# A two-block decoder on one core: the even mixer's order, low-rank gates of halves, and the order of shares and maxima in the sparse attention

## The chip, the cores and the metric

One core of one Trainium2 chip runs the whole program in one launch. The metric is the device time of that core in microseconds, the median over runs.

## The reference

Two blocks are computed for 512 tokens of width 1024, batch 1, all in float32. The first has two layers: an even mixer (a gMLP half and a gated delta net half), an MLP of width 4096 with squared relu, a gated addition of a side input, then the same with a differential attention as the mixer. The second has a gated linear attention (GLA) and a sparse attention (NSA). What matters here:

```python
# even mixer: spatial gate, conv + silu of q,k,v, l2 norms, chunked delta rule, out-projection
s = einsum('gts,bnsgc->bntgc', w, layer_norm(v)) + b_s ;  a_out = gelu(u) * s
v_new = u_c - w_c @ state ;  o_c = q_c @ state + qk_c @ v_new ;  state = state * g_last + k_c.T @ v_new
# GLA: a gate of rank 16 (16 columns of the projection, then 16 x 512), heads of 128/256
gk = log_sigmoid(glr @ w_gk_up + b_gk) / 16
o = rms_norm_2(gla_chunked(q, k, v, gk), head_norm) * silu(z) ;  y = o @ w_out
# NSA: per head three softmaxes (compressed keys, selected keys, window), gated and added
o = sum_c gates[c] * softmax(mask_c(q @ k_c.T)) @ v_c ;  y = (o * silu(z)) @ w_out
```

## The kernel before

Every engine has its own hand-ordered program; semaphores join them. Dense products are made of float32r halves: ScalarE rounds a piece of weights to its upper half (`act_weights`, WH), VectorE subtracts to get the lower half (`dve_weights`, WL), and TensorE adds three products (upper x upper, upper x lower, lower x upper) for each pair of tiles. A unit of weights is 1 MB in one of two raw buffers, loaded by the queue of SyncE in the order of `weight_plan`; a unit makes two parts, and a part has one of three WH/WL slots. So part j can be rounded once part j-3 has been used, and the place where `act_weights(a, j)` and `dve_weights(v, j)` stand in the engines' programs decides when it is. `feat` makes 128 output features for all 512 tokens (24 matmuls of 512 columns); `feat_slowly` makes the same in pieces of 8 matmuls, to be put beside other work; `toks` makes 512 output features for the four token tiles, in four PSUM banks. `several` makes a few float32 matmuls into one bank. The eight banks are handed out in turn (`Banks.take`), unless a bank is named, and a bank's next user waits until its last one was read.

The even mixer (`pe_even`, `act_even`, `dve_even`, `pool_even`): ten `qkv` features with convolutions (three VectorE taps each), l2 norms (`pe_l2`, `act_l2`, `dve_l2`), four spatial gates (`pe_gate`, `dve_gate`), two `eu` features, values turned to token form (`vb`), the products `at` and `qk` with `dve_products`, then five doubling levels of an inverse (jobs `m` and `xy`, lines 1134 to 1158) with pieces of dense features beside them (`beside`), and a recurrence of four chunks n, into which `gm_product` puts the eight out-projections of the gMLP half. `head_norm`, `head_square`, `head_scale`, `head_gain`, `head_half` and `head_rest` finish a chunk's output. The second out-projection is `eo`, and the norm ahead of the MLP (`act_norm`, `dve_norm`) follows.

GLA (`pe_gla`, `act_gla`, `dve_gla`, `pool_gla`): the 16 gate columns are the job `gs`, copied to `GLR`; four float32 matmuls with 16 rows (`gup`) widen them. Per head h there are state updates (`values`), outputs, and `finish_head`, which sums two tiles of squares by two float32 matmuls with ones (lines 2122, 2123).

NSA (`pe_nsa`, `act_nsa`, `dve_nsa`, `pool_nsa`): 52 units u in two halves f; token tile q is 3, 2, 1, 0, and each (f, q) starts with one unit on compressed keys (branch None), then units on selected and window keys. In step i TensorE makes scores(i+2), turns shares(i) and multiplies values(i-1), and in the first half three steps of four also hold a dense piece. ScalarE copies half of the turned shares and makes the exponentials (i+2). VectorE's step (line 2914) is

```python
nsa_step(i, ((most, 2), (scale, 1), (turn_, 0), (mix, -1)))
```

that is, the row maxima of unit i+2, then the factors (gate over sum) of unit i+1, then its copy of half of turned unit i, then the mixing where a q ends; `split_` follows, and in some steps `z_gate` with a part of weights. GpSimd waits for the factors and multiplies the shares of unit i+1 (`share`), and TensorE's `turn_` waits for that. At the end the out-projection `yo` takes banks 0 to 3 and then 4 to 7, while the last three steps still run.

## Time and profile before

| what | value |
|---|---|
| median of 3 runs | 2063.66 us (2061.76 to 2064.04) |
| the profiled execution's own time | 2062.59 us |
| its span | 2060.4 us |
| mean granted TensorE clock | 0.996 |
| TensorE busy | 1980.1 us, 96% of the span |
| VectorE, ScalarE, GpSimd busy | 1069.3, 891.7 and 221.5 us |

The span is shown in stretches by stage: the even mixer takes about 16 to 314 us, GLA 1407 to 1650 us, NSA 1650 to the end. PE is TensorE, DVE VectorE, ACT ScalarE, POOL GpSimd. A float32 matmul counts as two instructions.

### The profile page before, as it was taken

How to read it: one execution, taken by the hardware profiler on the slowest of the kernel's cores; microseconds unless marked ns; L12 is line 12 of the kernel's file. 1: busy time of each engine (PE TensorE's matmuls, PEld its weight loads, DVE VectorE, ACT ScalarE, POOL GpSimd, SP SyncE). 2: the span in 40 equal slices, each digit the busy share in tenths (PEclk: the TensorE clock that was granted, in tenths of full speed). 3: DMA queues.
4: the chain of work that ended last, by engine and by line, in shares of the span. 5: the costliest groups of instructions: out<-in, count | busy, mean ns of one | idle time of the engine just before them, and what ended most of it. 6: DMA issues, size and time to landing. Idle time of an engine off the chain costs nothing.

```text
span 2060.4 us, 27307 instructions
## 1 busy us (share of the span) xinstructions
PE 1980.1 (96%) x11161; PEld 1592.5 (77%) x11161; DVE 1069.3 (52%) x1706; ACT 891.7 (43%) x1659; POOL 221.5 (11%) x225
## 2 busy tenths in 40 slices
PE   7999989999999999999999999999999989999888
PEld 6778878888888788656888888887887778966567
DVE  5576555434434552566543434356535656555763
ACT  5562244323223563666442323256434442355562
POOL 1011000000000000342000000000000034233440
PEclk9999999999999999999999999999999999999999
DMA  4221013333232322111332333223221155611002
GB/s 146 81 76 48 22 62 99 96 102 101 84 102 82 102 77 97 62 41 42 93 103 85 99 102 102 82 83 97 82 92 62 62 149 147 177 42 42 1 1 72
DMA packets 122945, 169.94 MB, mean 82 GB/s; under 512 B 7562, under 2 KB 83862, under 8 KB 122822
## 3 DMA queue, kind: packets, MB, share of 16 engines
q1 hardware_dynamic: 114966, 151.00, 23.2%
q0 software_dynamic: 5504, 14.58, 2.6%
q10 hardware_dynamic: 2352, 2.62, 0.4%
q8 instruction: 89, 1.46, 0.3%
q14 instruction: 34, 0.28, 0.0%
HBM read 158.22 MB, written 2.10 MB: 78 GB/s over the span
## 4 chain that ended last, share of the span: by engine, by line
PE 78%; DVE 9%; ACT 7%; issue 2%; POOL 1%; DMA 1%; DVEq 0%; SPq 0%; ACTq 0%
PE PSUM L520 59%; PE PSUM L558 6%; PE PSUM L528 5%; DVE WL L413 2%; ACT XN L430 2%; PE PSUM L535 2%; ACT WH L486 1%; ACT TM L430 1%; DVE AR L413 1%; ACT AR L430 1%; PE PSUM L2557 1%; DVE AR L421 1%; PE PSUM L2606 1%; DVE XL L413 1%; PE PSUM L2578 1%
## 5 line engine op out<-in xcount | busy, mean ns | idle before, releaser
L413 DVE TENSOR_TENSOR WL<-RAW,WH 128x1024 fp32r<-128x1024 f32 (+2 forms) x284 | 348.9, 1230 | 383.7 <-ACT WH L486 383.2
L486 ACT CAST WH<-RAW 128x1024 fp32r<-128x1024 f32 (+2 forms) x284 | 293.2, 1035 | 372.2 <-PE PSUM L520 366.5
L520 PE MATMUL PSUM<-XH,WH 128*128 128x512 f32 (+3 forms) x1120 | 414.9, 370 | 10.5 <-DVE XL L413 6.7
L520 PE MATMUL PSUM<-XH,WL 128*128 128x512 f32 (+3 forms) x1120 | 407.3, 364 | 0.0
L520 PE MATMUL PSUM<-XL,WH 128*128 128x512 f32 (+3 forms) x1120 | 407.2, 364 | 0.0
L520 PE MATMUL PSUM<-WH,HP 128*128 128x512 f32 x1024 | 318.0, 390 | 1.9 <-DVE WL L413 1.9
L520 PE MATMUL PSUM<-WH,XH 128*128 128x512 f32 (+2 forms) x608 | 239.1, 393 | 11.7 <-DVE WL L413 5.5
L520 PEld LDWEIGHTS PSUM<-XH,WH 128*128 128x128 f32 (+2 forms) x1120 | 209.3, 187 | 50.7 <-DVE XL L413 8.4
L520 PEld LDWEIGHTS PSUM<-XL,WH 128*128 128x128 f32 (+2 forms) x1120 | 209.3, 187 | 35.8 <-issue 2.9
L520 PEld LDWEIGHTS PSUM<-XH,WL 128*128 128x128 f32 (+2 forms) x1120 | 209.0, 187 | 34.1
L520 PE MATMUL PSUM<-WH,XL 128*128 128x512 f32 (+2 forms) x608 | 232.0, 382 | 0.0
L520 PE MATMUL PSUM<-WL,XH 128*128 128x512 f32 (+2 forms) x608 | 231.6, 381 | 0.0
L520 PEld LDWEIGHTS PSUM<-WH,HP 128*128 128x128 f32 x1024 | 192.2, 188 | 42.7 <-DVE WL L413 2.8
L430 ACT ACTIVATE TM<-PSUM 128x512 f32<-128x512 f32 x128 | 76.0, 598 | 312.0 <-PE PSUM L520 259.3
L520 PE MATMUL PSUM<-WL,HP 128*128 128x512 f32 x512 | 199.2, 389 | 0.0
L520 PEld LDWEIGHTS PSUM<-WH,XH 128*128 128x128 f32 x608 | 115.1, 189 | 39.0 <-DVE WL L413 8.1
L413 DVE TENSOR_TENSOR TM<-TM 128x512 f32<-128x512 f32 x70 | 48.5, 692 | 169.1 <-ACT TM L430 168.4
L520 PEld LDWEIGHTS PSUM<-WL,XH 128*128 128x128 f32 x608 | 115.2, 189 | 22.2 <-issue 2.2
L520 PEld LDWEIGHTS PSUM<-WH,XL 128*128 128x128 f32 x608 | 114.9, 189 | 21.9
L520 PEld LDWEIGHTS PSUM<-WL,HP 128*128 128x128 f32 x512 | 96.1, 188 | 19.8
L528 PE MATMUL PSUM<-AR 64*64 64x64 f32 (+6 forms) x1424 | 97.9, 260 | 7.6 <-ACT TM L430 3.5
L528 PEld LDWEIGHTS PSUM<-AR 64*64 64x64 f32 (+3 forms) x1424 | 74.4, 149 | 29.7 <-issue 20.1
(236 smaller groups left out, 2480.4 us busy)
## 6 DMA issues: line engine op xcount, KB each, us to landing
RAW<-in_w_mlp_dram SPq DMA_DIRECT2D x64, 1024.0 KB, 5.2
RAW<-in_nsa_w_in_dram SPq DMA_DIRECT2D x13, 1024.0 KB, 5.5
RAW<-in_w_in_e_dram SPq DMA_DIRECT2D x12, 1024.0 KB, 5.2
RAW<-in_w_qkv_o_dram SPq DMA_DIRECT2D x12, 1024.0 KB, 5.2
RAW<-in_gla_w_in_dram SPq DMA_DIRECT2D x12, 1024.0 KB, 5.3
RAW<-in_w_ple_gate_dram SPq DMA_DIRECT2D x8, 1024.0 KB, 5.0
RAW<-in_w_out_e_dram SPq DMA_DIRECT2D x4, 1024.0 KB, 5.0
RAW<-in_w_out_o_dram SPq DMA_DIRECT2D x4, 1024.0 KB, 5.0
```

Of the source, the lines that this page charges most:

```text
L413: return x.do.tensor_tensor(o, a, b, op)
L421: return x.do.scalar_tensor_tensor(out=o, in0=a, scalar=s, in1=b, op0=op0, op1=op1)
L430: return a.do.activation(o, i, func, **kw)
L486: a.do.copy(hi, r).then_inc(*up("w_hi", "w_hi", j))
L520: m = p.do.matmul(o, l, r, start=start and i == 0, stop=stop and i == len(pairs) - 1)
L528: m = p.do.matmul(o, l, r, start=True, stop=True)
L535: m = p.do.transpose(o, i, IDT[0:i.shape[0], 0:i.shape[0]])
L558: m = p.do.matmul(PS[bank], l, r, start=i == 0, stop=i == len(pairs) - 1)
L2557: p.do.matmul(o[r][:, nk * j:nk * j + nk], NQ[h, m0 + j, cs], (KS, KW)[br][h, (m0 + j) // 2, 0:nk], start=j == 0, stop=False, skip_group_c ...
L2578: x = p.do.transpose(o[:, 128 * (c * n + j):128 * (c * n + j) + 128], NSB[u % 3][:, r, nk * j + 128 * c:nk * j + 128 * c + 128], IDT)
L2606: x = p.do.matmul(o[64 * r:64 * r + 64, 128 * l:128 * (l + w)], (VS, VW)[br][:, c, 64 * g:64 * g + 64], PT[u % 2][:, r, 128 * (c * n + j): ...
```

## The change

Six places are edited; all else is the same.

1. Even mixer, gates: gate 3 goes behind the first `eu` feature, the two `eu` features take the named banks of qkv(2,3) and qkv(2,2), and the `vb` turns go behind both. VectorE takes gate 3 and the first product with `gu` ahead of `vb`.
2. Even mixer, levels: the eighteen pieces are dealt out so that level 5 has two between `m` and `xy`; the weights behind the last feature go behind the splits of the gMLP half.
3. Even mixer, recurrence: at n = 1 ScalarE rounds weights ahead of `head_scale`; VectorE's `head_gain` goes behind the next chunk's `RR`; the last products are put around `head_norm(2)`. In `eo`, weights are split up to one part less, but earlier.
4. GLA gate: the 16 columns are loaded three times, at 0, 32 and 64 of 80 columns; `UP` is cleared by GpSimd and loaded three times; ScalarE rounds both; VectorE subtracts to get `UPH[64:80]` and `GLR[32:48]`; the four `gup` matmuls are float32r with 80 rows.
5. GLA heads: VectorE adds the two tiles of squares, one matmul with ones is left, and `finish_head(h)` goes behind the next head's first `gz`.
6. NSA: `scale` ahead of `most`; the out-projection in other banks.

Semaphore names are also merged (`v_spread`, `v_stats`, `dt_a_log`, `gate_halves`), with the same waits.

```diff
-    S(w, 2048, 2064)
+    plan.append(("R", rows(w)[:, :, 2048:2064]))
...
+                if plan[u][0] == "R":
+                    for i in range(3):
+                        load(s, f"raw{u % NR}", ("raw", u) if i == 2 else (), raw_of(u)[:, :, 32 * i:32 * i + 16], plan[u][1])
+                    continue
...
-                if i in (8, 9):
-                    for g in (2 * i - 16, 2 * i - 15):
-                        pe_gate(p, g)
-            feat(p, ("eu", 0), EVEN)
+                if i == 8:
+                    pe_gate(p, 0)
+                    pe_gate(p, 1)
+                elif i == 9:
+                    pe_gate(p, 2)
+            feat(p, ("eu", 0), EVEN, bank=ps.where["qkv", 2, 3][0])
+            pe_gate(p, 3)
+            feat(p, ("eu", 1), EVEN, bank=ps.where["qkv", 2, 2][0])
             for n in range(4):
                 p.wait_ge(*at("qkv", 2, 3))
                 pe_token_form(p, "vb", n, VT)
-            feat(p, ("eu", 1), EVEN)
...
                     pe_token_form(p, "kd", lv - 1, KN)
+                else:
+                    beside(2)
...
-                if lv <= 4:
-                    beside(3 if lv == 1 else 2)
+                beside((2, 2, 2, 1, 0)[lv - 1])
...
-                gm_product()
-                if n:
-                    head_norm(n - 1)
+                if n < 3:
+                    gm_product()
+                    if n:
+                        head_norm(n - 1)
                 within(n)
+            head_norm(2)
+            gm_product()
             head_norm(3)
...
+                if n == 1:
+                    act_weights(a, first_part["eg", 0] + 4)
+                if n == 3:
+                    head_square(3)
                 if n:
                     head_scale(n - 1)
-                if n == 1:
-                    act_weights(a, first_part["eg", 0] + 4)
-            head_square(3)
...
                     for t in range(4):
                         act_half(a, MLP0, t)
+                        if t == 1:
+                            act_weights(a, j + 3)
...
             dve_gate(v, 2)
-            dve_gate(v, 3)
             dve_l2(v, 1, range(4))
...
             dve_weights(v, first_part["eu", 0] + 3)
+            dve_gate(v, 3)
+            gate(0)
             for n in range(4):
                 dve_token_form(v, "vb", n, VB, beta)
-            gate(0)
...
-                if lv == 4:
-                    dve_weights(v, first_part["ez", 3] + 3)
...
+                    if n > 1:
+                        head_gain(n - 2)
                     gm_add(*adds.pop(0))
...
                     for t in range(4):
                         add(t)
+                        if t == 2:
+                            dve_weights(v, j + 3)
                         dve_half(v, MLP0, t)
-                    dve_weights(v, j + 4)
...
-                several(p, ("gup", h), lambda b: [(b[:, :], UP[:, 128 * h:128 * h + 128], GLR)])
+                several(p, ("gup", h), lambda b: [(b[:, :], UPH[:, 128 * h:128 * h + 128], GLR)])
...
             def finish_head(h):
-                p.wait_ge(*at("gsq", h, 1))
-                b = ps.take("gn", h)
-                p.wait_ge(*ps.empty("gn", h))
-                p.do.matmul(PS[b][:, :], ONE, tm("gq", h, 0), start=True, stop=False)
-                p.do.matmul(PS[b][:, :], ONE, tm("gq", h, 1), start=False, stop=True).then_inc(*ps.filled("gn", h))
+                p.wait_ge(*at("gsq_sum", h))
+                several(p, ("gn", h), lambda b: [(b[:, :], ONE, tm("gq", h, 0))])
...
                     feat(p, ("gz", 2 + 2 * h), GLA)
+                    if h:
+                        finish_head(h - 1)
                     feat(p, ("gz", 3 + 2 * h), GLA)
                     values(h + 1)
                 outputs(h)
-                if h < 3:
-                    finish_head(h)
+            finish_head(2)
...
+            a.wait_ge(*at("gk_up"))
+            a.do.copy(UPH, UP).then_inc(*up("gate_halves", "up_hi"))
+            a.wait_ge(*ps.full("gs"))
+            a.do.copy(GLR, bank("gs")[0:80, :]).then_inc(*up("gate_halves", "glr_hi"))
...
+            g.wait_ge(*ps.full("pg", 1, 0, 0))
+            step(g, g.do.memset(UP, 0.0))
+            for i in range(3):
+                load(g, "gk_up", ("gk_up",) if i == 2 else (), UP[32 * i:32 * i + 16, :], I["gla_w_gk_up_2"][0])
...
-                 tiles=TILES[1], banks=(0, 1, 2, 3))
-            toks(p, ("yo", 1, 1), mixed_ready, tail=True, tiles=TILES[1], banks=(4, 5, 6, 7))
+                 tiles=TILES[1], banks=(2, 1, 0, MORE))
+            toks(p, ("yo", 1, 1), mixed_ready, tail=True, tiles=TILES[1], banks=(ACC, 5, 4, 3))
...
-                nsa_step(i, ((most, 2), (scale, 1), (turn_, 0), (mix, -1)))
+                nsa_step(i, ((scale, 1), (most, 2), (turn_, 0), (mix, -1)))
```

## Rows read from the trace of the kernel before

**Rows 1.** The page: the span, and busy time of TensorE (share, instructions).

```profile
span 2060.4 us, 27307 instructions
PE 1980.1 (96%) x11161; PEld 1592.5 (77%) x11161; DVE 1069.3 (52%) x1706; ACT 891.7 (43%) x1659; POOL 221.5 (11%) x225
```

**Rows 2.** Waits of TensorE, whole span: total us, times, longest.

```profile
PE PSUM L2578 <- POOL AR L413: 12.3, 19, 1.5
```

**Rows 3.** Stretches: us, busy PE, PEld, DVE, ACT, POOL, PEclk, DMA share, GB/s.

```profile
140.50:143.90 3.40, 3.25 (x9) 2.48 (x8) 2.65 (x5) 3.31 (x7) 0.00 (x0) 0.50 0.02 5
300.90:304.30 3.40, 3.40 (x10) 2.63 (x9) 1.17 (x2) 1.94 (x5) 0.00 (x0) 0.50 0.93 291
1441.00:1444.40 3.40, 3.40 (x9) 2.64 (x8) 0.90 (x2) 3.35 (x7) 0.00 (x0) 0.50 0.01 4
```

**Rows 4.** Gates to products: one stretch, then timeline of PE and DVE (start, us).

```profile
136.02:155.03 19.01, 15.41 (x73) 12.85 (x73) 13.65 (x17) 11.47 (x14) 0.00 (x0) 0.91 0.32 102
...
139.48 1.18 PE L528 MATMUL PSUM<-AR 128*128 128x128 f32 x8 [3.45 <-ACT TM L430]
...
134.45 2.32 DVE L421 SCALAR_TENSOR_TENSOR AR<-PSUM,COL,AR 128x511 f32<-128x511 f32 x3
...
168.15 0.43 DVE L413 TENSOR_TENSOR AR<-CS,AR 128x256 f32<-128x256 f32 x1
```

**Rows 5.** Timeline of PE, levels and recurrence of the even mixer.

```profile
227.81 7.37 PE L528 MATMUL PSUM<-AR 64*64 64x64 f32 x192 [1.20 <-DVE AR L413]
...
262.25 0.50 PE L520 MATMUL PSUM<-WH,XH 128*128 128x512 f32 x1 [1.76 <-DVE WL L413]
...
265.37 1.16 PE L528 MATMUL PSUM<-AR 128*128 128x128 f32 x8 [1.46 <-DVE AR L413]
...
283.85 1.12 PE L528 MATMUL PSUM<-TM,CB 128*128 128x512 f32 x2 [1.03 <-ACT TM L430]
```

**Rows 6.** Timeline of PE, out-projection `eo` and first MLP features; last, ACT.

```profile
299.63 0.50 PE L520 MATMUL PSUM<-WH,XH 128*128 128x512 f32 x1 [2.37 <-DVE WL L413]
299.96 0.39 PE L520 MATMUL PSUM<-WL,XH 128*128 128x512 f32 x1
300.19 0.40 PE L520 MATMUL PSUM<-WH,XL 128*128 128x512 f32 x1
...
314.85 0.36 PE L520 MATMUL PSUM<-XH,WH 128*128 128x256 f32 x1 [0.79 <-DVE XL L413]
...
313.85 1.04 ACT L486 CAST WH<-RAW 128x1024 fp32r<-128x1024 f32 x1
```

**Rows 7.** GLA gate: timeline of PE, then the DMA issue of its columns.

```profile
1436.80 3.69 PE L528 MATMUL PSUM<-AR 16*128 16x512 f32 x8
...
RAW<-in_gla_w_in_dram SPq DMA_DIRECT2D x1, 64.0 KB, 3.8
```

**Rows 8.** Timeline of PE, end of the first GLA head.

```profile
1555.48 1.13 PE L2122 MATMUL PSUM<-TM,CB 128*128 128x512 f32 x2 [0.69 <-ACT TM L430]
1556.44 1.02 PE L2123 MATMUL PSUM<-TM,CB 128*128 128x512 f32 x2
```

**Rows 9.** Timeline of one NSA step, second half, q 3: DVE, ACT, POOL, PE.

```profile
1937.21 1.99 DVE L413 TENSOR_TENSOR XL<-TM,XH 128x512 fp32r<-128x512 f32 x1
1939.13 1.21 DVE L2853 TENSOR_REDUCE ST<-PSUM 128x2 f32<-128x1024 f32 x1
1940.26 0.15 DVE L2885 RECIPROCAL ST<-ST 128x2 f32<-128x2 f32 x1
...
1936.45 0.69 ACT L430 ACTIVATE AR<-PSUM,ST 128x512 f32<-128x512 f32 x1 [0.38 <-DVE ST L2853]
...
1936.77 1.89 POOL L413 TENSOR_TENSOR AR<-AR,ST 128x1024 f32<-128x1024 f32 x1 [2.03 <-DVE ST L413]
...
1938.71 1.09 PE L2578 MATMUL PSUM<-CB,AR 128*128 128x128 f32 x8 [0.52 <-POOL AR L413]
```

**Rows 10.** Timeline of PE, start of NSA's out-projection.

```profile
2005.45 0.50 PE L520 MATMUL PSUM<-WH,XH 128*128 128x512 f32 x1 [2.81 <-ACT AR L430]
```

More of the change, by code:

```diff
@@ L1322, in z_gate @@
                 act(a, EZ[:, m, :], bank("ez", m)[:, :], ACT.Silu).then_inc(*ps.read("ez", m))
-                act_weights(a, first_part["ez", m] + 3)
+                if m < 3:
+                    act_weights(a, first_part["ez", m] + 3)
             def gate(m):
@@ L1347, in act_even @@
                     step(a, act(a, va, va, ACT.Ln, scale=1.0 / 128, bias=EPSC))
-                    act(a, va, va, ACT.Exp, scale=-0.5).then_inc(*up("v_scale", "v_scale"))
+                    act(a, va, va, ACT.Exp, scale=-0.5).then_inc(*up("v_spread", "v_scale"))
                     conv_silu(j, m)
@@ L2050, in bass_decoder_pair @@
         RS = CS[:, L_R:L_R + 512]
-        UP = slot(11)[0:16, 0:512]
-        GLR = slot(11)[0:16, 512:1024]
+        UP = slot(3)[0:80, 0:512]
+        UPH = PP[0:80, 0, 0, :]
+        GLR = PP[0:80, 0, 1, :]
+        SECOND, THIRD = slice(32, 48), slice(64, 80)
         PI = slot(11)[:, 1024:1536].bitcast(I32)
@@ L2209, in act_gla @@
                     gz(2 + 2 * h)
+                    if h:
+                        finish_head(h - 1)
                     gz(3 + 2 * h)
                 outputs(h)
-                if h < 3:
-                    finish_head(h)
                 if h == 2:
-                    for m in range(6):
+                    for m in range(4):
                         place(m)
             j = first_part["yo", 0, 0]
+            finish_head(2)
+            place(4)
+            place(5)
             finish_head(3)
@@ L2255, in dve_gla @@
             dve_weights(v, first_part["gs",] + 2)
-            v.wait_ge(*ps.full("gs"))
-            v.do.tensor_copy(GLR, bank("gs")[0:16, :]).then_inc(*ps.read("gs"))
+            v.wait_ge(*at("up_hi"))
+            tt(v, UPH[THIRD, :], UP[THIRD, :], UPH[THIRD, :].bitcast(F32), ALU.subtract).then_inc(*up("up_lo", "up_lo"))
+            v.wait_ge(*at("glr_hi"))
+            tt(v, GLR[SECOND, :], bank("gs")[SECOND, :], GLR[SECOND, :].bitcast(F32), ALU.subtract).then_inc(*ps.read("gs"))
             dve_weights(v, first_part["gs",] + 5)
@@ L2331, in values, with sum_squares @@
                 book.put(("g_state", h), f"bank{ps.where[job][0]}_read", ps.where[job][1])
+            def sum_squares(h):
+                v.wait_ge(*at("gsq", h, 0))
+                v.wait_ge(*at("gsq", h, 1))
+                tt(v, tm("gq", h, 0), tm("gq", h, 0), tm("gq", h, 1), ALU.add).then_inc(*up("gsq_sum", "gsq_sum", h))
             def finish_head(h):
@@ L2348, in dve_gla @@
                     gz(2 + 2 * h)
+                    if h:
+                        finish_head(h - 1)
                     gz(3 + 2 * h)
                     values(h + 1)
-                    finish_head(h)
+                sum_squares(h)
                 if h == 2:
-                    for m in range(6):
+                    for m in range(4):
                         place(m)
@@ L2373, in dve_gla @@
             j = first_part["yo", 0, 0]
+            finish_head(2)
+            place(4)
+            place(5)
             finish_head(3)
```

34 lines of the change are left out of this document (19 added, 15 removed).

## Prediction

> **What bounds the kernel now.** I read the page first: TensorE is busy 1980.1 of 2060.4 us [rows 1], so the kernel is TensorE's own work plus 80 us in which it stands still. A change can gain in three ways only: a wait of TensorE that goes, work of TensorE that goes, or a stretch at the lower clock that goes. Next I read TensorE's waits. The largest entry is 12.3 us in 19 waits for GpSimd [rows 2], all in the sparse attention. The rest I took one by one from TensorE's timeline, at the places that the diff touches; each row shows the idle time before it and what ended it. Last I read stretches for the granted clock. Three of 3.4 us show 0.50, which is 1.2 of 2.4 GHz [rows 3]: one behind 3.45 us of standing still, one behind 2.37 us, and one behind four matmuls that use 16 rows [rows 4, 6, 7]. At 0.50 half of the work of 3.4 us is lost, so each costs 1.7 us.
>
> **Even mixer, gates.** Gate 3 waited 3.45 us for ScalarE to read the l2 sum in its bank [rows 4]. Now the first `eu` feature stands ahead of it, in the bank of qkv(2,3), whose last reader is VectorE's third tap, which ends at 134.45 + 2.32 = 136.77 [rows 4]. TensorE was free at 136.02, so it waits 0.8 us. That takes 2.65 us off the stretch of 19.01 us [rows 4], and with a wait that short I expect the slow stretch behind it to go too, 1.7 us: 4.35. The second `eu` feature needs the bank of qkv(2,2), which is also gate 2's, read long before. VectorE doesn't gain as much: ahead of its products stand the same splits, four `vb` tiles and now gate 3 and one product. It gains about 3.2 us, and GpSimd's products with the decays come at the same time. Its last diagonal was ready at 168.6 [rows 4], some 0.7 us ahead of TensorE; TensorE being 4.35 us earlier, a new wait of 0.5 to 1 us arises. I take 0.8: net 3.5 us.
>
> **Levels.** The second half of level 5 waited 1.20 us for VectorE's masked product [rows 5], which was held behind a split of weights. Two pieces of 8 matmuls now lie between, 16 x 0.23 = 3.7 us by the spacing 299.96 to 300.19 [rows 6], and the split has gone behind. The wait goes: 1.2 us. They are taken from ends of levels 1 and 4, where two pieces and one remain, enough for VectorE's subtraction. The upper halves of the gMLP part begin later, as the last feature ends later, but behind them TensorE has 7.37 us of small matmuls [rows 5]: nothing.
>
> **Recurrence.** At n = 2 TensorE waits 1.76 us for lower halves and then 1.46 us for `RR` [rows 5]. Both come from ScalarE, which loaded a table and scaled head 0 before it rounded, and from VectorE, which took the gain of head 0 before `RR`. Turned about, both are on time; head 0's scale is 2 us later, and nothing waits for it until its place in the out-projection. At n = 3 the square of head 3 was waited for 1.03 us [rows 5]; a product of 2.7 us (12 x 0.23) now lies between. Sum 4.2 us.
>
> **Out-projection `eo`.** TensorE waited 2.37 us for the split of its last part, and the stretch at 0.50 follows [rows 6, 3]: 2.37 + 1.7 = 4.1 us. The price: the first part of the MLP was split here as well, and now isn't. ScalarE rounds it only behind its second turned tile, at 313.85 for 1.04 us [rows 6], VectorE then takes about 1.2 us, to 316.15, where TensorE began at 314.85 after 0.79 us [rows 6]. So 1.3 us comes back, and as 2.1 us of standing still may again be followed by the slow clock, I put 0.4 more. Net 2.4 us. Even mixer in all: 3.5 + 1.2 + 4.2 + 2.4 = 11.3 us.
>
> **GLA gate.** Four float32 matmuls took 3.69 us [rows 7]; as float32r of 512 columns they take 4 x 0.23 = 0.92. That is 2.8 us, and the slow stretch that follows them [rows 3] should go, as 80 rows now work: 1.7 us. Against it: rounding and splitting the gate columns takes 640 elements, not 128, on ScalarE and VectorE in the norm, where ScalarE is always busy. The bounds are nothing and the 1.04 us of a full part [rows 6]; by length 0.5 more, which I take in full. GpSimd's clearing of `UP` and two more loads lie on a queue that had nothing else to do in the MLP. SyncE issues three loads where one of 64 KB landed in 3.8 us [rows 7]; even in a row they end in 11.4 us, and a raw buffer is filled two units ahead, four parts or some 22 us of TensorE's work (4 x 24 x 0.23): nothing. Net 4.0 us.
>
> **GLA heads.** After each of three heads TensorE waited 0.69 us for the squares, then ran two matmuls, 0.96 us from start to start [rows 8]; by a `gup`, 3.69 / 4, I take 0.9 for one [rows 7]. Now a feature of 5.5 us covers squares and VectorE's addition, and one matmul is left: 3 x 0.69 + 4 x 0.9 = 5.7 us. With `finish_head(2)` behind head 3, outputs(3) loses 2.5 us of cover for VectorE's seven state updates and may wait 0.8 us; a wait of as much for the first split halves ahead of the out-projection goes in turn. Net 5.6 us. GLA: 9.6 us.
>
> **Sparse attention.** One step of the second half at q = 3 shows the ring. GpSimd's share runs 1936.77 to 1938.66, VectorE's XL subtraction beside it takes 1.99 us and ends at 1939.20, then come 1.21 us of maxima, 0.4 us of factors, and the next share at about 1940.7: 3.9 us [rows 9]. TensorE waits 0.52 us in it [rows 9], so alone it needs 3.4. With factors ahead of maxima, GpSimd starts 1.2 us earlier and the wait goes, if a new ring stays below 3.4: maxima 1.21, two exponentials 2 x 0.69, factors 0.4, signals 0.1, or 3.1 us [rows 9]. It does, barely. It doesn't where the exponentials are eight short ones, or where the compressed unit's four operations stand between; there some 0.8 us may stay at each of four changes of q without dense pieces. So of 12.3 us [rows 2] I take 9.5. The out-projection's first tile used bank 3 and waited 2.81 us for the last exponentials [rows 10]; in bank 7 it doesn't, and tiles 2, 1 and 0 come late enough: 2.8 us. NSA: 12.3 us.
>
> A VectorE subtraction of two SBUF tiles takes 1.99 us beside a share and ends just behind it [rows 9]. The Trainium skill, GPSIMD Engine Reference, section Specifications, says that GpSimd's SBUF interfaces are shared with VectorE, with contention for instructions with two SBUF inputs; the trace agrees. By that rule the change can lose: shares that start earlier fall on the compressed unit's subtraction, as the first rival has it.
>
> **Sum.** 11.3 + 9.6 + 12.3 = 33.2 us off the profiled execution's 2062.59 us: 2029.4. That execution is 1.1 us under the median, so I forecast 2031 us.
>
> **Rivals.**
> - *A: GpSimd holds VectorE.* The share now lies beside the maxima of the compressed unit and the splits, and those that read two SBUF tiles are stretched by up to 1.3 us (1.99 against 0.7) [rows 9], so the next maxima are late and TensorE waits as long as before. For it: the 1.99. Against it: maxima and copies read PSUM and keep their length. Only the 2.8 is gained: 2063.7 - 11.3 - 9.6 - 2.8 = 2040 us.
> - *B: new waits in the mixers.* Half of 20.9 us comes back, in VectorE's products, at state 3, before the MLP: 2063.7 - 10.4 - 12.3 = 2041 us. A and B together: 2051.
> - *C: everything goes well.* No residue at the changes of q (2.8 more), none in `eo` (1.7): 2026.
> - *D: slower.* VectorE now waits for the exponentials of unit i+1 before the maxima of i+2. If ScalarE's copy (about 0.6) and the share itself (1.89) come to stand in this ring, because the factors wait on both, a step takes 1.21 + 1.38 + 0.4 + 0.1 + 0.6 + 1.89 = 5.6 us against 3.9 [rows 9], 1.7 more in each of the 26 steps of the second half: 44 us. 2063.7 - 23.7 + 44 = 2084 us. It decides from 0.9 us a step (23.7 / 26). Against it: a share ends in TensorE's step before the factors of the next but one are wanted.
> - *E: no effect*, as TensorE's waits and clock only move: 2063.
>
> **How the numbers follow.** Forecast 0.55 (2027 to 2036 by its own terms), A 0.13, B 0.12, A and B 0.04, C 0.10, D 0.04, E 0.02. The range 2022 to 2046 takes in the forecast, A, B and C, 0.9 of the chance, which allows for sizes misjudged. Faster by over 0.2% (4.1 us, about what can be told from no change here) is 0.94, within it 0.02, slower 0.04.
>
> **What would show it.** In the profile after: no wait over 1 us before gate 3, clock 1.00 there and behind `gup`; `gup` 0.9 us; no wait at level 5 or n = 2; a wait of about 2 us before the first MLP feature; no GpSimd waits at q = 3 in the second half, and under 3 us of them in all; the out-projection starting without one. If TensorE's waits for GpSimd stay near 12 us, A holds; if VectorE waits for exponentials in most steps and steps take over 3.9 us, D does.

## The result, and the profile after

The changed kernel takes 2026.42 us (median of four, 2025.94 to 2026.63) against 2062.71 us before in the same comparison: a ratio of 0.9825, with a 95% interval of 0.9808 to 0.9842. Its profiled execution took 2026.30 us, with a span of 2024.5 us. The forecast was 2031 us, in a range of 2022 to 2046.

The page after, its span and busy times, to be held against [rows 1]:

```profile
span 2024.5 us, 27299 instructions
PE 1967.3 (97%) x11149; PEld 1589.8 (79%) x11149; DVE 1069.7 (53%) x1711; ACT 893.3 (44%) x1661; POOL 223.2 (11%) x228
```

Of the 35.9 us by which the span is shorter, 12.8 are busy time of TensorE and 23.1 are time in which it stood still. The other engines do as much as before: it is all order, four shorter matmuls, four left out, and the clock.

TensorE's waits after (total us, times, longest). The first line answers to [rows 2]:

```profile
PE PSUM L526 <- DVE WL L413: 9.1, 10, 2.8
...
PE PSUM L2624 <- POOL AR L413: 4.2, 7, 1.0
...
PE PSUM L2603 <- ACT AR L430: 1.3, 2, 0.7
```

12.3 us in 19 waits for GpSimd have become 4.2 us in 7; two waits for ScalarE at the scores are new.

To see where the rest came off, I laid the two PE timelines beside each other and took the time between the same matmul in both, at points where the work is the same. The distance grows from 0.5 us at 118 us (the first transfers, which vary from run to run) to 14.8 us at the end of the first MLP norm's first wait (314.85 before, 300.02 after), of which 1.4 are given back in the next 350 us, since at 0.50 the start of the MLP is slower here. It is 13.4 us all through the MLPs and the odd mixer, 23.5 us from the linear attention's out-projection to the sparse attention's features (1669.99 and 1646.50), and 35.9 at the end. Less the 0.5 us at 118 us, the even mixer gave 12.9 us, the linear attention 10.1, the sparse attention 12.4; forecast were 11.3, 9.6 and 12.3.

Four stretches of the trace after (columns as in [rows 3]):

```profile
139.00:142.40 3.40, 3.40 (x18) 2.85 (x18) 2.04 (x4) 3.33 (x6) 0.00 (x0) 1.00 0.00 0
...
300.68:304.09 3.41, 3.41 (x19) 3.41 (x18) 2.66 (x5) 3.31 (x8) 0.00 (x0) 0.50 0.39 90
1424.00:1428.00 4.00, 4.00 (x19) 3.31 (x18) 2.92 (x4) 1.90 (x3) 0.00 (x0) 1.00 0.80 262
1635.30:1638.71 3.41, 3.41 (x19) 3.41 (x18) 3.31 (x5) 3.31 (x7) 0.00 (x0) 0.50 0.00 0
```

The first and the third are the places of the gates and of `gup`, where the clock was 0.50 before [rows 3] and is 1.00 now. Half clock stands in two others: behind the wait for the first MLP feature, and at the start of the sparse attention. The second costs nothing. The next wait behind it, for VectorE's lower halves, is shorter by as much (PE timelines before and after):

```profile
1669.99 0.36 PE L520 MATMUL PSUM<-XH,WH 128*128 128x256 f32 x1 [1.19 <-DVE XL L413]
...
1646.50 0.36 PE L526 MATMUL PSUM<-XH,WH 128*128 128x256 f32 x1 [0.50 <-DVE XL L413]
```

From the end of the wait of 2.78 us ahead of the stretch to these matmuls it is 12.60 us before, all at full clock, and 12.62 us after, with 3.41 us at 0.50.

The PE timeline after, at the places of [rows 4 to 7], with VectorE's split at 298.55 and its tap at 133.99 between:

```profile
136.45 0.47 PE L526 MATMUL PSUM<-XH,WH 128*128 128x512 f32 x1 [0.88 <-DVE AR L421]
...
133.99 2.32 DVE L421 SCALAR_TENSOR_TENSOR AR<-PSUM,COL,AR 128x511 f32<-128x511 f32 x3
...
164.66 0.68 PE L534 MATMUL PSUM<-CB,AR 64*64 64x64 f32 x16 [0.26 <-DVE AR L413]
...
231.12 0.50 PE L526 MATMUL PSUM<-WH,XH 128*128 128x512 f32 x1 [1.42 <-DVE XL L413]
...
300.02 0.36 PE L526 MATMUL PSUM<-XH,WH 128*128 128x256 f32 x1 [2.08 <-DVE WL L413]
...
298.55 1.22 DVE L413 TENSOR_TENSOR WL<-RAW,WH 128x1024 fp32r<-128x1024 f32 x1
...
1423.71 1.09 PE L534 MATMUL PSUM<-PP 80*128 80x512 f32 x4
1424.64 0.40 PE L526 MATMUL PSUM<-XH,WH 128*128 128x512 f32 x1
...
1575.70 0.49 PE L2135 MATMUL PSUM<-AR 128*128 128x128 f32 x2 [0.76 <-DVE AR L421]
```

Gate 3's 3.45 us are down to 0.88 us, behind VectorE's third tap, which ends at 136.31. The new wait for VectorE's products is 0.26 us. The waits of 1.20, 1.76, 1.46, 1.03 and 2.37 us [rows 5, 6] have no successor; what is left there is 1.42 us at 231.12, which stood before as well (at 236.60), and 2.08 us before the MLP. The four `gup` matmuls take from 1423.71 to 1424.64, 0.93 us. The third state of the linear attention is waited for 0.76 us.

One step of the sparse attention in the second half at q = 3 (timelines of POOL, DVE and PE), and the first matmul of its out-projection, which answer to [rows 9, 10]:

```profile
1903.19 1.89 POOL L413 TENSOR_TENSOR AR<-AR,ST 128x1024 f32<-128x1024 f32 x1 [1.18 <-DVE ST L413]
1906.27 1.89 POOL L413 TENSOR_TENSOR AR<-AR,ST 128x1024 f32<-128x1024 f32 x1 [1.18 <-DVE ST L413]
...
1904.77 0.86 DVE L413 TENSOR_TENSOR XL<-TM,XH 128x512 fp32r<-128x512 f32 x1
...
1906.10 1.22 DVE L2899 TENSOR_REDUCE ST<-PSUM 128x2 f32<-128x1024 f32 x1
...
1903.09 1.09 PE L2652 MATMUL PSUM<-AR 128*64 128x128 f32 x16
...
1906.27 1.09 PE L2652 MATMUL PSUM<-AR 128*64 128x128 f32 x16
...
1969.48 0.50 PE L526 MATMUL PSUM<-WH,XH 128*128 128x512 f32 x1
```

Shares start every 3.07 to 3.08 us, and TensorE's step takes 3.18; before, both took 3.92. No wait stands in the step, and none before the out-projection.

### The profile page after: what moved, and what is told of

The parts are those of the page before. It is cut to its first block, busy times and chain, and to the rows that moved or that the text cites. A ratio compares the mean times of both kernels' runs of the same rounds, so it can differ in the third digit from the quotient of the medians.

```text
span 2024.5 us, 27299 instructions
## 1 busy us (share of the span) xinstructions
PE 1967.3 (97%) x11149; PEld 1589.8 (79%) x11149; DVE 1069.7 (53%) x1711; ACT 893.3 (44%) x1661; POOL 223.2 (11%) x228
## 3 DMA queue, kind: packets, MB, share of 16 engines
q8 instruction: 89, 1.46, 0.3%
## 4 chain that ended last, share of the span: by engine, by line
PE 80%; DVE 9%; ACT 7%; issue 3%; DMA 0%; SPq 0%; DVEq 0%; ACTq 0%
PE PSUM L526 63%; PE PSUM L564 5%; PE PSUM L534 5%; ACT AR L430 2%; ACT XN L430 2%; DVE AR L413 1%; PE PSUM L541 1%; DVE WL L413 1%; DVE AR L421 1%; DVE ST L2899 1%; ACT WH L492 1%; ACT TM L430 1%; PE PSUM L2603 1%; DVE XL L413 1%; PE PSUM L2652 1%
## 5 line engine op out<-in xcount | busy, mean ns | idle before, releaser
L526 PE MATMUL PSUM<-XH,WH 128*128 128x512 f32 (+3 forms) x1120 | 415.0, 371 | 13.4 <-DVE XL L413 6.1
L413 POOL TENSOR_TENSOR AR<-AR,ST 128x1024 f32<-128x1024 f32 (+2 forms) x52 | 81.5, 1567 | 135.9 <-DVE ST L413 135.9
L534 PE MATMUL PSUM<-AR 64*64 64x64 f32 (+5 forms) x1416 | 93.9, 258 | 0.8 <-ACT AR L1418 0.8
```

Source lines behind the costliest of these rows:

```text
L413: return x.do.tensor_tensor(o, a, b, op)
L526: m = p.do.matmul(o, l, r, start=start and i == 0, stop=stop and i == len(pairs) - 1)
L534: m = p.do.matmul(o, l, r, start=True, stop=True)
```

## The experiments

Every kernel below is the changed one with the edit shown. They were run in three groups, each beside the kernel before: the two NSA orders, the old banks and the early split (before: 2065.32 us), the four mixer edits put back (2064.33), and the changed kernel once more with the split in the gap, both improvements and the compressed-unit order in old banks (2064.65). Differences to the changed kernel are taken from its 2026.42 or 2026.18 us. Those between groups carry some uncertainty: the kernel before moved from 2062.71 to 2065.32 between them. The profiles also differ from the changed kernel's first one by -1.1 to +0.9 us at 22 us already, where no edit has come into play, so where a cost is read from two traces, I take it inside the edited stage, from the same matmuls in both.

### The changed kernel once more

> The changed kernel itself, once more, as the measure for the three beside it on the same chip, and to see which of its 3.4 us stretches at half clock stay where they are. In the ten profiles read so far, TensorE stands still before the first MLP feature for 2.1 us in eight, and a stretch at 0.50 follows in five of these. Theory 1: whether one follows a wait is chance; then the five runs show mean clocks that differ by up to 0.002 and times that differ by one or two times 1.7 us, 2026 to 2030 us. Theory 2: it is fixed by the kernel: the stretches stand at about 300.7, 1635.3 and at the end again, and all times agree within 1 us.

2026.18 us (2025.97 to 2027.56, four runs), ratio 0.9819 (0.9806 to 0.9833). Two stretches of its trace:

```profile
231.78:235.19 3.41, 3.41 (x10) 2.66 (x9) 0.18 (x1) 0.40 (x2) 0.00 (x0) 0.50 0.00 0
300.68:304.09 3.41, 2.74 (x23) 2.77 (x24) 3.19 (x6) 2.26 (x6) 0.00 (x0) 1.00 0.03 8
```

The same kernel with the same waits (1.42 and 2.06 us) has its half clock behind the first of them this time, and full clock behind the second. The stretch at 1634.66 is in both. So the place isn't fixed by the kernel, though the sum hardly differs: theory 1 holds for the place, and the times lie within 1.6 us, not much more than the 1 us of theory 2. Over the fourteen profiles of this study the stretch behind the 1.42 us wait is there in seven. The wait of 2.1 us before the first MLP feature stands in ten of them, and a stretch follows in six; in nine of these ten exactly one of the two places has it. The Trainium skill, TensorE: Matmul & The Clock Gate, Part 1, says of a kernel's start that the number of slow matmuls differs between runs of one kernel. These two traces show the like in the middle of a kernel: 19 matmuls at 0.50 from 300.68 us in one, 10 from 231.78 us in the other.

### Maxima first again, new banks kept

```diff
-                nsa_step(i, ((scale, 1), (most, 2), (turn_, 0), (mix, -1)))
+                nsa_step(i, ((most, 2), (scale, 1), (turn_, 0), (mix, -1)))
```

> The changed kernel with one line put back: in the sparse attention VectorE takes the maxima of unit i+2 before the factors of unit i+1 again; the new banks of the out-projection stay. My theory: the order alone gave 9.5 us in the prediction, and in the trace TensorE's waits for GpSimd fell from 12.3 to 4.2 us while 1.3 us of new waits for ScalarE at the scores came up, so 7 to 9.5 us come back: 2033.5 to 2036 us, with waits of about 0.5 us for GpSimd at every step of q = 3 in the second half. Rival: the banks were what counted (the exponentials' banks come free earlier), and the order alone is worth under 3 us: 2027 to 2029 us.

2035.82 us (2035.29 to 2036.46), 9.4 us over the changed kernel. The spans (2034.7 and 2024.5) differ by 10.2, but 0.8 of it stands at 22 us already; inside the sparse attention it is 9.4, with 0.63 at a wait for lower halves at 1727 that this order doesn't explain. VectorE's split of a mixed tile at q = 3 takes 2.00 us again, at 1914.35. Its waits for GpSimd:

```profile
PE PSUM L2624 <- POOL AR L413: 12.5, 19, 1.5
```

The 19 waits are back to the count, and my theory holds: it said 7 to 9.5 us. A wait costs more than its own length: TensorE's step is 3.92 us with 0.53 of waiting and 3.18 without.

### The old banks, new order kept

```diff
-                 tiles=TILES[1], banks=(2, 1, 0, MORE))
-            toks(..., tiles=TILES[1], banks=(ACC, 5, 4, 3))
+                 tiles=TILES[1], banks=(0, 1, 2, 3))
+            toks(..., tiles=TILES[1], banks=(4, 5, 6, 7))
```

> The changed kernel with the out-projection's banks put back, tiles 3, 2, 1, 0 in banks 3, 2, 1, 0 and then 7, 6, 5, 4; the order of factors and maxima stays. My theory: its first tile waits 2.8 us again for the last exponentials to be read, nothing else moves, and a wait of that length may be followed by 3.4 us at half clock, 1.7 us more: 2029 to 2031 us. Rival: with the factors ahead of the maxima the last exponentials are early enough, and the banks are worth under 1 us: 2026.4 to 2027.4 us.

2034.11 us (2033.66 to 2034.30), 7.7 us over the changed kernel, and 8.0 by the traces, all of it inside the sparse attention. I expected 2.8 to 4.5. PE and DVE timelines, then the stretch:

```profile
1975.78 0.80 PE L526 MATMUL PSUM<-WH,XH 128*128 128x512 f32 x1 [5.62 <-ACT AR L430]
...
1966.98 1.23 DVE L2899 TENSOR_REDUCE ST<-PSUM 128x8 f32<-128x1024 f32 x1
```

```profile
1972.76:1979.59 6.83, 3.81 (x9) 3.05 (x10) 1.00 (x4) 3.41 (x17) 3.29 (x3) 0.50 0.01 3
```

The wait is 5.62 us, not the 2.81 of [rows 10], and 6.83 us at half clock go with it, of which 3.8 are work (1.9 lost; with 5.62 that is 7.5 of the 8.0). VectorE takes the factors of the last compressed unit (1965.50 to 1967.07) ahead of the maxima at 1966.98, and so the exponentials behind them are late. That is a price of the new order which I had not seen, and the new banks hide it. Both theories fall.

### Maxima first at the compressed units only

```diff
+                if i + 1 < NT and n_at[i + 1][2] is None:
+                    nsa_step(i, ((most, 2), (scale, 1), (turn_, 0), (mix, -1)))
+                else:
+                    nsa_step(i, ((scale, 1), (most, 2), (turn_, 0), (mix, -1)))
-                nsa_step(i, ((scale, 1), (most, 2), (turn_, 0), (mix, -1)))
```

> The changed kernel, but where unit i+1 is a compressed one (the first of each q, its factors are four operations of VectorE behind one of GpSimd's share) the maxima of i+2 stand ahead of the factors again; everywhere else the factors stand ahead. Theory 1: the 0.94 us for which TensorE waits at 1898, just behind a compressed unit, comes from maxima that are held behind these four operations; ahead of them they are 1.9 us earlier, and some 0.5 us are gained at each of three or four changes of q: 2024.4 to 2026 us. Theory 2: TensorE turns the compressed unit itself before the next one, so what is gained there is lost at its own turn, which now waits 0.6 us for its share: 2026 to 2028 us. Theory 3: the order of the compressed units was as much of the gain as the rest: 2029 us or more.

2024.23 us (2023.98 to 2024.68), 2.0 to 2.2 under the changed kernel, and faster than either order taken throughout. The two were not run side by side; inside the sparse attention the traces differ by 2.1. Its waits for GpSimd:

```profile
PE PSUM L2624 <- POOL AR L413: 1.5, 2, 1.0
...
PE PSUM L2619 <- POOL AR L413: 0.9, 2, 0.6
```

4.2 us have become 2.4. Theory 1 holds, with a little more than it asked; of theory 2 there are two waits, 0.31 and 0.59 us, for the compressed unit's own share. The wait of 1.04 us at 1892, behind eight short exponentials, stays.

### The same with the old banks

The edit of the section before, and `banks=(0, 1, 2, 3)` and `banks=(4, 5, 6, 7)` in the out-projection.

> The sparse attention with maxima ahead only where unit i+1 is a compressed one, and the out-projection in the old banks. It tells why the banks were worth 5.6 us of waiting with the new order, and 2.8 us with the old. My theory: with the factors ahead everywhere the maxima of the last unit but one stand behind the four operations of the compressed unit, and the last exponentials end 5.6 us behind the point where TensorE wants their bank; with maxima ahead there, they end at 1971.9 us where TensorE is free at 1967.9 us in the trace with the new banks, so it waits 4.0 us, and 3.4 to 6.8 us at half clock may follow: 2030 to 2032.5 us. Rival: the wait is set by the number of exponentials alone and stays 5.6 us: 2032 to 2034 us.

2030.13 us (2028.79 to 2031.27). The out-projection's first matmul:

```profile
1971.60 0.79 PE L526 MATMUL PSUM<-WH,XH 128*128 128x512 f32 x1 [3.86 <-ACT AR L430]
```

3.86 us where I had worked out 4.0, in place of 5.62. My theory holds: 1.8 us of the wait came from the maxima behind the compressed unit. What is left over the 2.81 of before, 1.05 us, is the order as well, in the last step, as the last scores and the maxima of these scores show (PE and DVE, this kernel, then before):

```profile
1965.66 0.60 PE L2606 MATMUL PSUM<-CS 128*128 128x512 bf16 x2
1967.07 0.20 DVE L2931 RECIPROCAL ST<-ST 128x8 f32<-128x8 f32 x1 [0.93 <-ACT AR L430]
1967.39 1.22 DVE L2899 TENSOR_REDUCE ST<-PSUM 128x8 f32<-128x1024 f32 x1
...
2000.52 0.60 PE L2560 MATMUL PSUM<-CS 128*128 128x512 bf16 x2
2001.23 1.22 DVE L2853 TENSOR_REDUCE ST<-PSUM 128x8 f32<-128x1024 f32 x1 [0.20 <-PE PSUM L2560]
```

Before, the maxima start 0.71 us after the start of the last scores' matmuls. Here they start 1.73 us after it, since the factors of the unit before stand ahead of them and wait for its exponentials. That is 1.02 of the 1.05 us. Maxima first in the last step too, with the old banks, was not run. Here too 6.83 us at half clock stand by the wait.

### The first MLP split, one addition too early

```diff
                            dve_weights(v, j + 3)
                        dve_half(v, MLP0, t)
+                    dve_weights(v, j + 4)
```

> The changed kernel, and VectorE also splits the first part of the MLP's weights behind the fourth addition of the first half of the even mixer's out-projection, where it stands still for 1.35 us and ScalarE has rounded that part 1.2 us before. My theory: the wait of 2.08 us before the first MLP feature is this split alone; it falls to the 0.7 us that the second turned tile's lower halves set, and the stretch at half clock behind it goes as well, 1.7 us: 2.6 to 3.1 us less, 2023.3 to 2023.8 us. Rival 1: the wait shrinks but the stretch at half clock stays, as at other places it also follows waits that are no longer than this: 1.3 us less, 2025.1 us. Rival 2: VectorE is late by one split with the norm of the first tiles and the wait only changes its cause: 2026 to 2027 us.

2027.41 us (2025.42 to 2032.53), just past the 2026 to 2027 of rival 2, and four executions that spread by 7 us decide little; so I go by the trace, which is of the fastest. PE, then DVE:

```profile
291.85 1.09 PE L541 MATMUL PSUM<-CB,XN 128*128 128x128 f32 x8 [1.86 <-ACT XN L430]
...
287.90 1.23 DVE L413 TENSOR_TENSOR WL<-RAW,WH 128x1024 fp32r<-128x1024 f32 x1 [0.79 <-ACT WH L492]
```

Rival 2: of the wait before the MLP 0.49 us is left, but the addition stands behind the split, at 289.04, the first tile's scale behind the addition, and TensorE waits 1.86 us for that.

### The same split in VectorE's gap

```diff
                    tt(v, o, o, bank("eo", c, t)[:, :], ALU.add).then_inc(*ps.read("eo", c, t))
+                    if c and t == 0:
+                        dve_weights(v, j + 2)
```

> The changed kernel, and VectorE splits the first part of the MLP's weights right behind the first addition of the second half of the even mixer's out-projection. One addition earlier the same split only exchanged a wait of 2.08 us before the first MLP feature for one of 1.86 us before the first turned tile, as the addition was late. Theory: in the gap of 1.35 us in which VectorE waits for the first tile's scale the 1.22 us cost nothing; the wait falls to about 0.8 us, that is 1.3 us less than the kernel beside it, and 3.0 us less where the stretch at half clock behind it goes as well. Rival: the split is still too long for the gap, the first tile is turned later, and the waits together stay near 2 us: within 0.5 us of it.

2024.03 us (2023.01 to 2024.69), 2.15 under the changed kernel beside it. PE, then DVE:

```profile
299.00 0.36 PE L526 MATMUL PSUM<-XH,WH 128*128 128x256 f32 x1 [0.77 <-DVE XL L413]
...
287.67 1.22 DVE L413 TENSOR_TENSOR WL<-RAW,WH 128x1024 fp32r<-128x1024 f32 x1
289.10 0.49 DVE L417 TENSOR_SCALAR XN<-H,ST 128x512 f32<-128x512 f32 x1 [0.22 <-ACT ST L430]
```

The split ends at 288.89, before the scale is there, and the wait is 0.77 us. That is 1.3 us; the other 0.85 lies between nothing and the 1.7 of one stretch, of which this trace has one less than the changed kernel's.

### Both improvements

> The changed kernel with two more edits: VectorE takes the maxima ahead of the factors where unit i+1 is a compressed one (alone its profile was 1.6 us shorter, with 2.4 us less of waiting for GpSimd), and it splits the first part of the MLP's weights behind the first addition of the second half of the out-projection. Theory: the two lie in different stages and add up: 1.3 to 3 us for the split and 1.6 to 3 us for the order, 3 to 6 us less than the changed kernel beside it. Rival: what is saved at the waits comes back as stretches at half clock at other places: under 2 us less.

2021.74 us (2020.37 to 2022.30, five runs), ratio 0.9795 (0.9782 to 0.9808), 4.4 us under the changed kernel beside it and 42.9 under the kernel before. The single gains were 2.0 and 2.15: they add up. Beside the split alone, run in the same group, the order of the compressed units gives 2.3 us, so that gain doesn't rest on a comparison between groups. This is the fastest version found.

### The gates put back

```diff
-                if i == 8:
-                    pe_gate(p, 0)
-                    pe_gate(p, 1)
-                elif i == 9:
-                    pe_gate(p, 2)
-            feat(p, ("eu", 0), EVEN, bank=ps.where["qkv", 2, 3][0])
-            pe_gate(p, 3)
-            feat(p, ("eu", 1), EVEN, bank=ps.where["qkv", 2, 2][0])
+                if i in (8, 9):
+                    for g in (2 * i - 16, 2 * i - 15):
+                        pe_gate(p, g)
+            feat(p, ("eu", 0), EVEN)
...
+            feat(p, ("eu", 1), EVEN)
...
             dve_gate(v, 2)
+            dve_gate(v, 3)
...
-            dve_gate(v, 3)
-            gate(0)
             for n in range(4):
                 dve_token_form(v, "vb", n, VB, beta)
+            gate(0)
```

> The changed kernel with the even mixer's gates put back: all four gates ahead of the first eu feature, the eu features in banks of their own choice, VectorE's value tiles ahead of its first gate product. My theory: the wait of 3.45 us ahead of gate 3 comes back for the two short ones that stand there now (0.88 and 0.26 us), 2.3 us, and with it the stretch at half clock behind it, 1.7 us: 4.0 us, 2030 to 2031 us. Rival: a stretch at half clock belongs to the work in it (small matmuls), not to the wait ahead, and is not changed by this: 2.3 us, 2028.5 to 2029 us.

2032.22 us (2031.65 to 2033.01), 6.0 us over the changed kernel. PE timeline, and two stretches:

```profile
138.54 0.71 PE L534 MATMUL PSUM<-AR 128*128 128x128 f32 x4 [3.44 <-ACT TM L430]
```

```profile
139.35:142.76 3.41, 3.41 (x11) 2.60 (x10) 2.55 (x4) 3.31 (x6) 0.00 (x0) 0.50 0.00 0
234.92:238.33 3.41, 3.41 (x10) 2.64 (x9) 0.71 (x1) 0.93 (x3) 0.00 (x0) 0.50 0.00 0
```

The wait of 3.44 us and the half clock behind it are both back, as my theory has it, which said 2.3 + 1.7 = 4.0. The second stretch is the one that the changed kernel has sometimes here, sometimes at the MLP. Inside the even mixer this kernel loses 4.1 us by the traces. The median of 2032.22 is over the theory's 2030 to 2031 us all the same. In the profile a further 1.7 us are lost in the sparse attention, at two waits in code that the edit doesn't touch: 0.89 us at 1730.20 for VectorE's lower halves and 0.57 us at 1771.54 for ScalarE. They come and go between profiles: the changed kernel's two have neither, the first stands in four others with 0.32 to 0.71 us, and the profile before has both. Why stays open.

### The low-rank gate put back

The core of the edit; the loads, GpSimd's clearing and ScalarE's copies go back with it.

```diff
-    plan.append(("R", rows(w)[:, :, 2048:2064]))
+    S(w, 2048, 2064)
...
-        UP = slot(3)[0:80, 0:512]
-        UPH = PP[0:80, 0, 0, :]
-        GLR = PP[0:80, 0, 1, :]
+        UP = slot(11)[0:16, 0:512]
+        GLR = slot(11)[0:16, 512:1024]
...
-                several(p, ("gup", h), lambda b: [(b[:, :], UPH[:, 128 * h:128 * h + 128], GLR)])
+                several(p, ("gup", h), lambda b: [(b[:, :], UP[:, 128 * h:128 * h + 128], GLR)])
...
-            tt(v, GLR[SECOND, :], bank("gs")[SECOND, :], GLR[SECOND, :].bitcast(F32), ALU.subtract)...
+            v.do.tensor_copy(GLR, bank("gs")[0:16, :]).then_inc(*ps.read("gs"))
```

> The changed kernel with the low-rank gate of the linear attention put back: four float32 matmuls with 16 rows, one copy of VectorE, loads of 16 rows and columns. My theory: the four matmuls take 3.7 us again in place of 0.9, the stretch at half clock behind them comes back (1.7 us), and the 0.42 us that rounding and splitting cost in the norm goes: 4.1 us, 2030 to 2031 us. Rival 1: the stretch at half clock came from the waits of the norm before it and does not come back: 2.4 us, 2028.5 to 2029 us. Rival 2: the features behind the gate wait for VectorE or ScalarE, which cover the longer matmuls: under 1.5 us, 2026 to 2028 us.

2031.22 us (2030.78 to 2033.13), 5.0 over. PE timeline and stretch:

```profile
1423.68 4.20 PE L528 MATMUL PSUM<-AR 16*128 16x512 f32 x8
```

```profile
1426.75:1433.58 6.83, 6.83 (x16) 4.51 (x15) 3.44 (x7) 6.65 (x12) 0.00 (x0) 0.50 0.15 52
```

The profiled execution is the slowest of the four (2033.13). From 1393 to 1609 us it loses 5.6 us. 6.83 us at half clock cost 3.4, the four matmuls 2.8, and 0.4 come back in the norm, where the wait of 0.78 us before the gate columns is gone. Rivals 1 and 2 fall; the half clock behind these matmuls is as real as I took it, and here twice as long. It starts while they run, and TensorE's last wait, of 1.06 us, ended at 1407.33, 19 us earlier. Whether the 16 rows bring it, or the float32 format and the 3.7 us that come with them, isn't shown: the edit changes all three.

### Two matmuls for a head's norm

```diff
-                p.wait_ge(*at("gsq_sum", h))
-                several(p, ("gn", h), lambda b: [(b[:, :], ONE, tm("gq", h, 0))])
+                p.wait_ge(*at("gsq", h, 1))
...
+                p.do.matmul(PS[b][:, :], ONE, tm("gq", h, 0), start=True, stop=False)
+                p.do.matmul(PS[b][:, :], ONE, tm("gq", h, 1), start=False, stop=True)...
...
-                sum_squares(h)
```

> The changed kernel, but the norm of each of the four heads of the linear attention sums its two halves with two accumulating matmuls again, and VectorE does not add them first; the place of the norm, behind the next feature, stays. It tells the two parts of that edit apart. My theory: each matmul left out is worth 0.9 us, as the prediction has it by the float32 matmuls of the gate: 3.6 us, less up to 0.5 us of waits that VectorE's additions cause: 2029.5 to 2030.2 us. Rival: beside a feature's matmuls the second one takes its columns at the full rate, 0.23 us each: 0.9 us, 2027.3 us.

2030.62 us (2029.59 to 2031.10), 4.4 over. By the PE timelines 3.5 us of it lie between 1407 and 1609 us, 0.88 for each of the four:

```profile
1543.62 1.02 PE L2148 MATMUL PSUM<-TM,CB 128*128 128x512 f32 x2
1544.48 1.02 PE L2149 MATMUL PSUM<-TM,CB 128*128 128x512 f32 x2
```

The 0.9 us holds, and the rival's 0.23 doesn't. So of the 5.6 us forecast for the heads, 3.5 are matmuls; the 2.1 for the covered squares rest on the three waits of 0.69 us that are gone [rows 8], and were not run by themselves. The 0.9 us between 3.5 and 4.4 lie outside this stretch and belong to nothing that I found.

### The recurrence put back

The core of the edit, for TensorE (the third product and the norm of head 2), ScalarE and VectorE:

```diff
-                if n < 3:
-                    gm_product()
-                    if n:
-                        head_norm(n - 1)
+                gm_product()
+                if n:
+                    head_norm(n - 1)
...
-                if n == 1:
-                    act_weights(a, first_part["eg", 0] + 4)
                 if n:
                     head_scale(n - 1)
+                if n == 1:
+                    act_weights(a, first_part["eg", 0] + 4)
...
-                    if n > 1:
-                        head_gain(n - 2)
...
+                if n:
+                    head_gain(n - 1)
```

> The changed kernel with the recurrence of the even mixer put back: ScalarE loads and scales before it rounds at n = 2, VectorE takes the gain of the head before ahead of the residual, the third product and the norm of head 2 in their old place. My theory: three waits of 1.76, 1.46 and 1.03 us come back, 4.2 us: 2030 to 2031 us. Rival 1: as TensorE now comes to this part relatively earlier against the other engines, the waits are longer and one of them is followed by 3.4 us at half clock: 2032 us or more. Rival 2: the wait of 2.08 us before the first MLP feature takes part of them in, since the norm that it waits for is no later: 2027 to 2029 us.

2034.48 us (2034.37 to 2034.63), 8.3 over. PE timeline and stretch:

```profile
256.26 0.50 PE L526 MATMUL PSUM<-WH,XH 128*128 128x512 f32 x1 [1.76 <-DVE WL L413]
...
259.38 0.58 PE L534 MATMUL PSUM<-AR 128*128 128x128 f32 x1 [1.26 <-DVE AR L413]
...
280.23 0.70 PE L534 MATMUL PSUM<-TM,CB 128*128 128x512 f32 x1 [1.04 <-ACT TM L430]
```

```profile
257.60:264.43 6.83, 5.57 (x25) 5.05 (x24) 2.29 (x4) 1.59 (x3) 0.00 (x0) 0.50 0.40 150
```

The three waits are back, 4.1 us, no longer than before, and half clock with them, 6.83 us with 5.57 us of work, of which half is lost, 2.8. So of rival 1, which gave 2032 us or more, the half clock holds and the longer waits don't. Up to the first MLP feature this kernel loses 7.5 us, so 0.6 are left, or 0.2 for each wait, by an estimate. The kernel before had much the same waits without half clock. So the edit is worth 4.1 us by its waits, and 2.8 more where it also keeps the clock up.

## Why the prediction was right

**Even mixer, gates.** Right in kind and nearly in size. The wait before gate 3 is 0.88 us (0.8 forecast), the stretch is gone, and putting the order back costs both. The new wait at the products is 0.26 us, not 0.8: VectorE had more room than I gave it.

**Levels and recurrence.** No wait at level 5, at n = 2 or at n = 3. The levels' edit was not run by itself; its 1.2 us rests on the two traces. The recurrence's waits measured 4.1 us against the 4.2 of the forecast.

**`eo`.** The 2.37 us went and 2.08 us stand before the MLP, as worked out (0.79 + 1.3). That the split of the first MLP part is the whole of it is shown by its place in VectorE's gap, where 0.77 us are left. I counted 0.4 for the slow clock behind it; it came in one of two profiles of the same kernel, at the price of the stretch at 231, which stood in the profile before as well and which I left out of the sum. The profile before also has half clock at 236, where it costs 1.4 us by the two timelines, and the changed kernel's first profile hasn't; the half clock at the MLP costs 1.4 us and not the 0.4 put down for it. So of the 1.6 us by which 12.9 is over 11.3, 0.4 are these two, 0.5 are the products, and 0.7 are booked to no wait. This stage came out near the forecast partly by luck, since the clock's place isn't fixed.

**GLA.** Forecast 9.6 us, measured 10.1, term by term: `gup` 0.93 us for 0.92; the norm 0.4 us longer for 0.5 (from 1407.08 to 1420.44 before, 13.36 us; from 1393.61 to 1407.39 after, 13.78 us); a head's matmul 0.88 for 0.9; the wait at outputs(3) 0.76 for 0.8. The stretch behind `gup` is gone, and comes back with the old matmuls; the reason that I gave for it, that 80 rows work in place of 16, isn't shown by itself.

**Sparse attention.** 12.4 us for 12.3, but the two terms are not what I said they were. Inside this stage, the order undone costs 9.4 us (9.5 forecast), the banks undone 8.0 (2.8 forecast). So of the 12.4 the order alone would have given 4.4 and the banks alone 3.0; these two are differences, and neither was run. The step that failed is the one that took the out-projection's 2.81 us as independent of the order. With the old banks, the new order makes that wait 5.62 us: 1.76 by the compressed unit's factors ahead of the last maxima but one, 1.05 by the factors ahead of the last ones. Half clock comes on top. The sum was right because both edits are in the change, and the new banks hide what the order would cost.

The ring came out at 3.07 us against the 3.1 of the forecast, but TensorE's own step is 3.18, not 3.4: a wait also costs some 0.2 us beyond its length. The residues of GpSimd are 4.2 us rather than 2.8, and 1.3 us of waits for ScalarE at the scores are new, which takes that back. That these errors cancel to 0.1 us is luck. The sign of under 3 us of GpSimd waits was missed, and the 2.8 was also a slip: four changes of q at 0.8 us are 3.2. Two of the residues, 1.04 and 0.95 us, stand where I put them (eight short exponentials, the compressed unit's operations), and the second went when maxima stood first there.

**The rivals.** A (2040) has no part in it: its price even fell, as the split of a mixed tile takes 0.86 us in place of 1.99, because the share now ends early in it. The rule of the Trainium skill, GPSIMD Engine Reference, section Specifications, still shows elsewhere: the compressed unit's subtraction of 128x256 takes 1.27 us inside a share, where it takes 0.42 us beside none. B (2041) has three small parts, 0.26, 0.76 and 2.08 us, all in the sum. C (2026) has the time almost to the point, but not the reasons: it wanted no residue at the changes of q and none in `eo`, and there are 4.2 and 2.08 us. The measured 2026.42 is even just under the 2027 to 2036 that the forecast's own terms span, by what the even mixer gave over its share. E (2063) falls. D (2084) would have needed steps of 5.6 us, and there are 3.2.

## What to carry to other kernels

When two edits touch the same chain of waits, cost each one with the other already made: here they gave 12.4 us together, and by difference 7.4 us one by one. An operation that is moved ahead in a loop should be looked at in each kind of iteration, since the kind with the longer work (here the compressed unit) may want the old order; that was worth some 2 us. And a piece of work without a hurry goes into a gap that is longer than it is, not to the nearest early place: one addition too early, the same split gained a fifth of a microsecond of waiting in place of 1.3.

## What the runs showed of the hardware

The half clock, 1.2 of 2.4 GHz, came where I had not looked for it. Stretches of 3.41 us at 0.50 followed waits of TensorE of 1.42 us in seven of fourteen profiles, and of 2.1 us in six of ten, at the same place in the same kernel in one execution and not in the next. Behind 5.62 and 3.86 us, and in the recurrence with 1.76 and 1.26 us close together, 6.83 us stood at 0.50. Behind the four float32 matmuls with 16 rows it came with no wait just ahead, 3.41 us in one kernel and 6.83 in the other. And at the start of the sparse attention it cost nothing, as a wait behind it was shorter by as much. A wait that goes can so be worth its length, or 1.7 us and more on top, and single profiles that differ by this much can't tell which. It also means that a stretch that is gone from one profile, as the one at 236 us from the changed kernel's first, may be back in the next.

TensorE's step in the sparse attention shrank by 0.74 us when a wait of 0.52 us went. Most of the 0.2 us between them is in how a wait is booked. The two bf16 matmuls ahead of it have a record of 0.28 or 0.29 us (PE timelines, before and after):

```profile
1937.90 0.29 PE L2560 MATMUL PSUM<-CS 128*128 128x128 bf16 x2
...
1905.17 0.28 PE L2606 MATMUL PSUM<-CS 128*128 128x128 bf16 x2
1905.29 1.04 PE L2624 MATMUL PSUM<-CB,AR 128*128 128x128 f32 x8
```

Without a wait the next matmuls start 0.12 us behind their start, with it 0.81 us (1937.90 to the 1938.71 of [rows 9]): 0.69 us later for 0.52 us of waiting, which is counted from the end of the record.

A VectorE subtraction of two SBUF tiles of 128x512 takes 0.69 us alone. In the sparse attention it took 1.99 us where 1.45 of it lay beside a share of GpSimd, and 0.86 where 0.32 did: 0.55 us beyond the overlap in both, so that it hardly moves on while the share runs. Maxima (1.22 us) and copies (0.68 us), which read PSUM, keep their length inside a share.

What stays open is what decides between two places for a stretch at half clock; no run here was made to settle that.
